# The first three products of some tiles move 272 columns, not 256

## The reference

```python
hl = modulate(rms_norm(xl, norm1_g[l]), mod_l[0], mod_l[1])
zl = hl @ w_in[l] + b_in[l]                     # 2048 x 13312, in pieces
g_conv, g_sgu, g_att = jnp.split(jax.nn.sigmoid(z[..., G_OFF:]), N_BRANCH, axis=-1)
xl = xl + mod_l[2] * ((g_conv * y_conv + g_sgu * y_sgu + g_att * y_att) @ w_o + b_o)
hl2 = modulate(rms_norm(xl, norm2_g[l]), mod_l[3], mod_l[4])
xl = xl + mod_l[5] * sq_relu_ffn(hl2, w_ff1, b_ff1, w_ff2, b_ff2)
# then on 272 tokens: differential attention (w_ain, w_aout), and a pooling
# mixer (w_pin, w_grp, w_pout), each with a norm before and after
```

## Time and profile before

| | |
|---|---|
| median of 3 runs | 2723.61 us (2723.15 to 2725.39) |
| profiled execution, device time | 2728.85 us |
| profiled execution, span of its instructions | 2726.8 us |
| TensorE busy | 2666.2 us, 98% of the span |
| VectorE busy | 1907.9 us, 70% |
| ScalarE busy | 1275.3 us, 47% |
| DMA | 539.00 MB, mean 198 GB/s |

### The profile page before, as it was taken

How to read it: one execution, slowest core, us unless ns; L and a number is a source line. 1 busy time by engine, 2 the same in 40 slices (tenths; PEclk the granted TensorE clock), 3 DMA queues, 4 the chain that set the end, 5 groups by cost and what they waited for, 6 DMA issues and landing times.

```text
span 2726.8 us, 51256 instructions
## 1 busy us (share of the span) xinstructions
PE 2666.2 (98%) x21400; PEld 2546.1 (93%) x21400; DVE 1907.9 (70%) x2865; ACT 1275.3 (47%) x1852; POOL 152.3 (6%) x162
## 2 busy tenths in 40 slices
PE   7999999999999999999999999999999999999998
PEld 4599977899999999989999999999999999989997
DVE  6766789889897788897555555577666665478564
ACT  5522344455446445554443544564444444554453
POOL 0000011100014000100000000030000000100000
PEclk9999999999999999999999999999999999999999
DMA  8766765465556788777555655654434444535553
GB/s 309 288 227 230 233 189 172 144 203 183 186 184 190 241 283 280 253 259 256 195 193 194 195 193 196 198 194 152 158 127 160 148 153 142 178 122 190 185 193 131
DMA packets 163989, 539.00 MB, mean 198 GB/s; under 512 B 31024, under 2 KB 35120, under 8 KB 163632
## 3 DMA queue, kind: packets, MB, share of 16 engines
q1 hardware_dynamic: 163760, 535.73, 59.0%
HBM read 533.57 MB, written 2.10 MB: 196 GB/s over the span
## 4 chain that ended last, share of the span: by engine, by line
PE 88%; DVE 7%; DMA 2%; ACT 1%; issue 1%; SPq 1%; DVEq 0%; POOL 0%; ACTq 0%
PE ps L575 26%; PE ps L580 26%; PE ps L577 26%; DVE lo L1713 2%; DMA raw<-in_w_ff 1%; PE ps L791 1%; PE ps L810 1%; PE ps L738 1%; PE ps L726 1%; PE ps L799 1%; DMA raw<-in_w_mod 1%; DVE row L2310 1%; PE ps L971 0%; ACT hi L1090 0%; PE ps L993 0%
## 5 line engine op out<-in xcount | busy, mean ns | idle before, releaser
L1090 ACT ACTIVATE hi<-raw 128x1024 fp32r<-128x1024 f32 x856 | 900.7, 1057 | 878.5 <-PE ps L580 458.6
L1713 DVE TENSOR_TENSOR lo<-raw,hi 128x1024 fp32r<-128x1024 f32 x856 | 1039.8, 1227 | 213.2 <-ACT hi L1090 211.8
L580 PE MATMUL ps<-AH,lo 128*128 128x256 f32 (+2 forms) x3504 | 992.7, 283 | 14.2 <-DVE lo L1713 14.2
L575 PE MATMUL ps<-AH,hi 128*128 128x256 f32 (+2 forms) x3504 | 1002.5, 286 | 2.7 <-DVE AL L2127 2.7
L577 PE MATMUL ps<-AL,hi 128*128 128x256 f32 (+2 forms) x3504 | 992.2, 283 | 0.0
L575 PEld LDWEIGHTS ps<-AH,hi 128*128 128x128 f32 x3504 | 662.4, 189 | 32.0 <-issue 29.9
L580 PEld LDWEIGHTS ps<-AH,lo 128*128 128x128 f32 x3504 | 662.7, 189 | 17.8 <-DVE lo L1713 17.8
L577 PEld LDWEIGHTS ps<-AL,hi 128*128 128x128 f32 x3504 | 662.7, 189 | 0.9
L580 PE MATMUL ps<-YH,lo 128*128 128x256 f32 (+1 forms) x1512 | 420.9, 278 | 0.9 <-DVE lo L1713 0.8
L575 PE MATMUL ps<-YH,hi 128*128 128x256 f32 (+1 forms) x1512 | 421.1, 279 | 0.0
L577 PE MATMUL ps<-YL,hi 128*128 128x256 f32 (+1 forms) x1512 | 421.0, 278 | 0.0
(11 more groups left out here) (287 smaller groups left out, 2948.6 us busy)
## 6 DMA issues: line engine op xcount, KB each, us to landing
raw<-in_w_ff SPq DMA_DIRECT2D x256, 512.0 KB, 4.2
raw<-in_w_in SPq DMA_DIRECT2D x208, 512.0 KB, 4.2
raw<-in_w_mod SPq DMA_DIRECT2D x192, 512.0 KB, 4.9
raw<-in_w_ain SPq DMA_DIRECT2D x128, 512.0 KB, 3.7
raw<-in_w_pin SPq DMA_DIRECT2D x64, 512.0 KB, 3.5
raw<-in_w_o SPq DMA_DIRECT2D x32, 512.0 KB, 4.7
raw<-in_w_aout SPq DMA_DIRECT2D x32, 512.0 KB, 3.5
raw<-in_w_pout SPq DMA_DIRECT2D x32, 512.0 KB, 4.0
```

Source lines behind the costliest of these rows:

```text
L575: e.matmul(b.ap[:, o], hi[:, k, :], xh, start=start and k + i == 0, stop=False, skip_group_check=many)
L580: mm = e.matmul(b.ap[:, o], los[j % NSPLIT][:, k, :], xh, start=False, stop=stop and k == KU - 1, skip_group_check=many)
L1090: e.activation(his[u % NSPLIT][:, :, :], raws[raw_at[i]][:, :].rearrange("p (k m) -> p k m", k=KU), ACT.Copy).then_inc(s_hi, 1)
L1713: e.tensor_tensor(los[u % NSPLIT][:, :, :], raws[raw_at[i]][:, :].rearrange("p (k m) -> p k m", k=KU), his[u % NSPLIT][:, :, :].bitcast(F3 ...
```

## The change

`unit` gets a flag, `broken`. It is set by a mean over 256 tokens (and cleared by one over 272), by the transposes that end a modulation block, and by a tile that had to wait block by block. The next tile that starts afresh, waits for nothing, and takes its operands from `lat`, `br`, `mixed` or `normal` then moves 272 columns instead of 256 in the three products of its first block, and clears the flag. The 16 extra columns are the first 16 of block 1; their sums go into columns 256 to 271 of the PSUM bank, which nothing reads. The values in the first 256 columns are the same.

```diff
+                more = broken and start and ready is None and parts in (lat, br, mixed, normal)
+                broken = broken and not more
...
-                    many = len(parts(0)) > 1
-                    for i, (xh, xl, o) in enumerate(parts(k0 + k)):
+                    many = len(parts(k0 + k)) > 1
+                    for i, (xh, xl, o) in enumerate(parts(k0 + k, T + 16) if more and k == 0 else parts(k0 + k)):
...
+                if ready is not None:
+                    broken = True
...
                 xb.free = (s_root, MEAN[key] + 1) if key != "s2" else (s_l1, 1)
+                broken = n == T
...
-            lat = lambda k: [(A1H[:, k, :], A1L[:, k, :], slice(0, T))]
+            def rows(h, l):
+                return lambda k, n=T: [(*(t[:, :, :].rearrange("p k t -> p (k t)")[:, T * k:T * k + n] for t in (h, l)),
+                                        slice(0, n))]
+
+            lat, br, mixed, normal = rows(A1H, A1L), rows(BH, BL), rows(Y1H, Y1L), rows(NH, NL)
...
                 mm.then_inc(s_modt, 1)
+                broken = True
```

More of the change, by code:

```diff
@@ L552, in _ @@
             s0, s1, tb, xb = Bank(S0), Bank(S1), Bank(TB), Bank(XB)
-            unit_at, tile_at = -1, 0
+            unit_at, tile_at, broken = -1, 0, False
             def opened(b):
@@ L560, in unit @@
             def unit(b, k0, parts, start, stop, ready=None):
-                nonlocal unit_at
+                nonlocal unit_at, broken
                 unit_at += 1
                 j = unit_at
+                more = broken and start and ready is None and parts in (lat, br, mixed, normal)
+                broken = broken and not more
                 for nb in mod_ends(j):
@@ L585, in gemm @@
             def gemm(parts, free, n=2, ready=None):
-                nonlocal tile_at
+                nonlocal tile_at, broken
                 b = opened(bank[tile_at % 4])
@@ L638, in mean @@
             def mean(key, n, total=ssum, last=None):
+                nonlocal broken
                 opened(xb)
@@ L888, in sgu_rest @@
                     tick()
-            br = lambda k: [(BH[:, k, :], BL[:, k, :], slice(0, T))]
             for n in range(3):
@@ L900, in _ @@
                 tick()
-            mixed = lambda k: [(Y1H[:, k, :], Y1L[:, k, :], slice(0, T))]
             for m in range(16):
@@ L916, in n2 @@
                 mean("n2", T, last=ADD["n2"] + 16)
-            normal = lambda k: [(NH[:, k, :], NL[:, k, :], slice(0, T))]
             spawn(n2())
```

## The result

The changed kernel takes 2748.52 us, median of 4 runs (2747.28 to 2750.13), against 2723.47 us (2723.15 to 2725.39) for the kernel before, timed again beside it: the ratio is 1.0091 (1.0073 to 1.0108), 25 us slower. The forecast was 2709.2 us. What happened in the long stretch is the third rival, though its time of 2732.5 us is 16 us too low as well: it counted on the 14.4 us of the sum.

The account below looks back on a forecast made before the run. TensorE's products times the distance between starts bound the kernel, at 113.3 or 117.8 ns. Gains of 7.7, 3.35, 1.7, 1.6 and 0.4 us, less 0.4 for width, took 14.4 from 2723.6 to 2709.2 us; range 2705 to 2725.

Parts of the forecast that it names:

- the third rival: Feed-forward from 1258.26 us: last wide triple knocks the quick stretch slow, 23.3 us lost, 2732.5 us in all; chance 0.13.
- the 14.4 us of the sum: Whole kernel: gains of 14.75 us from slow stretches turned quick, less 0.4 us for the width.
- the upper bound: At the wide tiles: each of the 19 starts a quick stretch, 113.3 instead of 117.8 ns per product; taken for the forecast.
- the lower bound: At the wide tiles: the wide triple sets the phase anew by chance and quick stretches are lost; not taken.
- Eleven of the 19 tiles ... gain nothing: Tiles at 310.71 to 473.11, 840.98, 994.42 to 1043.84 and 1183.70 to 1258.26 us: already in quick stretches, no gain.
- their terms: Parts of the predicted gain for the slow stretches, each 0.038 of the time to the next interruption.
- the stretches that the forecast counts on: Slow stretches from 640.05, 857.76, 945.93 and 1082.47 us, expected to turn quick: gains of 7.7, 3.35, 1.7 and 1.6 us.
- the prediction's 0.4 to 0.7: The 57 products widened to 272 columns: 7.2 or 11.7 ns more each, 0.4 to 0.7 us in all; 0.4 taken.
- rival 1: First long stretch, from 640 us: TensorE catches up with `lo` in DVE's bursts, stalls, turns slow; 2715 us; chance 0.20.
- Rival 2: Behind the wide tiles: slow rhythm returns at once or only one distance exists, only width is paid; 2724 us; chance 0.15.

Follow-up runs that it names:

- `scan_count`: Changed kernel without its 19 triples; some 96 feed-forward tiles instead start with 1 to 6 or 9 products of 272 columns, in mixed order: 2748.33 us, one run.
- `two_more`: Changed kernel with two wide products at blocks 0 and 4 instead of the triple, at the 19 tiles and three more: 2716.55 us, ratio 0.9957 to the kernel before.
- `no_last`: Changed kernel without its last wide triple, in the feed-forward; the other 18 stay: 2725.88 us, ratio 0.9988 to the kernel before.

## Why the prediction was wrong

**What bounds the kernel: right.** Products times distance, in two rhythms at one granted clock, held in every trace. The Trainium skill ("TensorE: Matmul & The Clock Gate", Back-to-back issue gap) gives one distance for a width. It calls that formula the isolated gap of a single matmul, and for a stream of pairs of weight load and matmul it states two other figures, 81 ns for 128 columns and 131 for 512, and none for 256. The trace disagrees with the formula: the stretches of all 14 traces have 113.3 or 117.8 ns for 256 columns, where the formula's estimate is 109.2.

**The step that failed** is this one: "I take the upper one, being nearest to those rows", with the upper bound "each of the 19 tiles starts a quick stretch". I had starts behind small products and one 258-column product, in none of which the delay came out of a running quick stream, and read from them that a long step always leads to quick. `scan_count` shows a map: the triple takes S0 and S1 to Q, and Q and S2 to S0. In the trace after all nine triples inside a run of products follow it: Q to S0 at 638.80, 906.04, 1076.99 and 1252.38 us, S2 to S0 at 522.08 and 1037.06 us, and S0 to Q at 774.49, 987.25 and 1177.78 us. The words for this were in the prediction, as "the lower bound", that it "sets the phase anew by chance"; only it isn't chance.

The rule failed behind interruptions too, where it had been read. Of the ten triples right behind one, five are followed by slow products (at 308.98, 339.85, 544.96, 1028.47 and 1210.84 us), and four of these starts were quick before. At 1028.47 us the first distance is 0.21 us and the next 0.13, both "long":

```profile
1028.47 0.37 PE L577 MATMUL ps<-BH,hi 128*128 128x272 f32 x1
1028.68 0.29 PE L579 MATMUL ps<-BL,hi 128*128 128x272 f32 x1
1028.81 0.28 PE L582 MATMUL ps<-BH,lo 128*128 128x272 f32 x1
```

The next 8.00 us hold 68 products, 117.6 ns each:

```profile
1029.00:1037.00 8.00, 8.00 (x70) 8.00 (x69) 7.41 (x13) 2.83 (x5) 0.00 (x0) 1.00 0.69 217
```

The rows had a warning: three of the four starts behind a mean, with 305 to 307 ns, were slow, so that "all slow starts come from short distances" was not true of them.

**"Eleven of the 19 tiles ... gain nothing"** was the same error in the sum. They were entered as zero (the forecast's 0 in the table of the result); each is a place where a quick stream can be lost, and the last has 587 us behind it. A kick into a stream that is quick already can only cost.

**Rival 3: right in the mechanism and size of its loss, wrong in its chance and in its sum.** It gave 23.3 us for the long stretch, measured 23.0 (from 1258.6 to 1845.7 us in the trace of before). Its 2732.5 us is 16 us too low, for it set the 14.4 us against it. It had 0.13. The argument against it ("from a long one every start went quick") counted starts in another condition than the one that mattered, and the two ways of entering weren't kept apart.

**The 14.4 us: mis-sized.** Up to the last triple 4.7 us were won in the profiled pair beyond the 1.2 already there at 523 us. The three gains that came (2.4, 2.0 and 1.6 us) are within 0.1 us of their terms. With two pairs the stretches that the forecast counts on turned quick, and the way from 640.05 us to 1125 us took 471.8 us: 13.4 less than in the profile of before, near the terms' 14.35, but 6.4 less than in its shorter pattern. The medians fell by 5.2 (2721.72 to 2716.55). The profiled execution of before, 5 us above its median, was taken as typical in its pattern; that is the size that was wrong even for a kick that works. It is also why the change costs 25 us in medians but 18.4 in the profiled pair.

**Width and DVE: right.** The three steps over a triple add 19 ns to a slow stream (774.49 us: 126, 126 and 120 ns in the trace) and 33 to a quick one (638.80 us: 120, 125 and 128), so that 19 triples cost 0.4 to 0.6 us, as the prediction's 0.4 to 0.7. TensorE's waits for `lo` went from 8.2 to 9.0 us; with the forecast's stretches quick (`two_more`) the view of waits has

```profile
PE ps L583 <- DVE lo L1725: 8.1, 7, 2.9
```

so rival 1 did not happen, not even from 642 to 662 us, where DVE is busy for 19.61 of 20.00 us and TensorE for all of it. At 1072 us DVE came to 93% (37.14 of 40.00 us), not 96. Rival 2 is out: the slow rhythm doesn't come back behind a pair.

**What stays open.** What in TensorE holds the phase: the 192 ns load goes with the S phases, and no run tells whether it is cause or effect. Whether more columns act by their time alone or also by where they are read: the widths' lack of order isn't explained. And why the same program enters a stretch in another phase from one execution to the next; the distances of 201 and 207 ns behind the transposes are the last that the trace shows of it.

## What to carry to other kernels

If a long stream of equal products shows two distances in different stretches, ask of any disturbance what it does from each of the two, and weigh the stretch behind each place by its length; measure the map (some 100 kicks fit into one execution) before putting one in. A disturbance that is harmless from the good phase and used twice is worth more than one that is strong. And compare a profiled execution's pattern with more than one other before booking its slow stretches as a gain: where a stream has two rhythms, one profile is one draw of several.

## What the runs showed of the hardware

- TensorE's stream of weight load and 256-column product has four phases, one of 113.3 ns per product and three of 117.8 ns. Q held for 5184 products, S0 for 5194 (the kernel after), S1 for 4899 (`no_last`). The three differ in which of a block's three loads takes 192 instead of 188 ns.
- A wider product shifts the phase by a fixed map, which depends on width, number and place; one product of 258 columns is enough (Q to S0, 4 of 4).
- The unchanged kernel takes one rhythm or the other in the same stretch: from 655 to 825 us three traces of six are slow and three quick, and from 640 to 1125 us it takes 485.2 or 478.2 us. 5 of 28 timed executions are above 2745 us in one series, 2 of 23 and 1 of 13 in two others, none of 19 in a fourth; such an execution was traced of `no_last` (2746.26 us), and its feed-forward was slow; of the kernel before there is no such trace. With two pairs at the heads of the 19 tiles (or 22) 23 of 24 stayed below 2722.5 us; the other is the single run of 5466 us.
